# Packed bfloat16 masks, head constants loaded late, and the filter's decay formed on the chip

## The reference, cut to what matters

```python
def _hyena_filter(L, w1, b1, f1, w2, b2, f2, w3, b3, f3, w4):
    t01 = t / max(L - 1, 1)
    z = concatenate([t01[:, None], cos(ang), -sin(ang)], axis=-1)
    h = sin(f1 * (z @ w1 + b1)); h = sin(f2 * (h @ w2 + b2)); h = sin(f3 * (h @ w3 + b3))
    h = h @ w4                                        # (256, 2048)
    deltas = abs(linspace(min_decay, max_decay, HYENA_W))   # (1024,)
    window = exp(-t01[:, None] * deltas[None, :])     # (256, 1024)
    return h * tile(window, (1, 2))

def _block(s, mod, s0_f, s0_b, p):
    sh_a, sc_a, g_a, sh_f, sc_f, g_f = mod            # silu(c) @ w_mod + b_mod
    h = rmsnorm(s, norm_pre_mix) * (1.0 + sc_a) + sh_a
    out, s_f, s_b = mixer(h, s0_f, s0_b, p)           # conv_qkv, a_log, dt_bias, gdn_norm, conv_hy, hyena filter
    s = s + g_a * rmsnorm(out, norm_post_mix)
    h = rmsnorm(s, norm_pre_ffn) * (1.0 + sc_f) + sh_f
    return s + g_f * rmsnorm((silu(h @ w_gate) * (h @ w_up)) @ w_down, norm_post_ffn)
```

## Time and profile before

| | us |
|---|---|
| median of 3 runs | 1673.58 |
| lowest and highest | 1664.75, 1673.95 |
| the profiled execution: its time | 1674.84 |
| its span in the profile | 1673.2 |

### The profile page before, as it was taken

The page is one execution under the profiler, slowest core; times in us unless marked ns, Lnnn a source line. Parts: engine busy times, 40 slices in busy tenths (PEclk is TensorE's granted clock), DMA queues, the critical chain, the costliest instruction groups (busy, mean ns, idle before and its releaser), DMA issues.

```text
span 1673.2 us, 27006 instructions
## 1 busy us (share of the span) xinstructions
PE 1633.6 (98%) x10110; PEld 1410.9 (84%) x10110; DVE 1151.5 (69%) x1701; ACT 769.7 (46%) x1281; POOL 116.6 (7%) x214
## 2 busy tenths in 40 slices
PE   8899999999999999999999999999999999999998
PEld 3257899899998999999998888888888888888886
DVE  4645889899899987776777555555555555665665
ACT  1346564655645556433446444444444444334331
POOL 2000110111101010000110000000000000111110
PEclk9999999999999999999999999999999999999999
DMA  9995353443534445224993344454454456877872
GB/s 360 422 380 211 124 178 132 139 171 127 182 134 138 162 142 183 101 99 156 332 349 123 151 189 167 195 201 166 185 201 178 174 200 224 283 248 248 279 260 94
DMA packets 83305, 334.06 MB, mean 200 GB/s; under 512 B 8120, under 2 KB 24585, under 8 KB 56778
## 3 DMA queue, kind: packets, MB, share of 16 engines
q1 hardware_dynamic: 62592, 258.25, 41.9%
q0 software_dynamic: 19504, 68.20, 12.2%
q10 hardware_dynamic: 1114, 6.34, 1.0%
HBM read 328.56 MB, written 4.19 MB: 199 GB/s over the span
## 4 chain that ended last, share of the span: by engine, by line
PE 84%; DMA 7%; DVE 5%; ACT 2%; issue 1%; DVEq 1%; SPq 0%; ACTq 0%
PE g L485 10%; PE o L485 10%; PE o L478 8%; PE o L479 8%; PE o L480 8%; PE g L486 5%; PE o L486 5%; DMA w_mod_tile_o<-in_w_mod_t 4%; DMA w_mod_raw<-in_w_mod_t 3%; PE g L561 2%; PE o L492 2%; PE g L492 2%; PE o L493 2%; PE g L494 2%; PE o L494 2%; PE g L493 2%
## 5 line engine op out<-in xcount | busy, mean ns | idle before, releaser
L459 DVE TENSOR_TENSOR w_lo<-w_raw,w_hi 128x2048 fp32r<-128x2048 f32 x203 | 464.8, 2290 | 210.7 <-ACT w_hi L454 210.4
L454 ACT CAST w_hi<-w_raw 128x2048 fp32r<-128x2048 f32 x204 | 389.8, 1911 | 222.9 <-PE o L494 73.9
L478 PE MATMUL o<-h_hi,w_hi 128*128 128x256 f32 (+1 forms) x896 | 298.1, 333 | 3.2 <-DVE w_lo L459 1.8
L480 PE MATMUL o<-h_hi,w_lo 128*128 128x256 f32 (+1 forms) x896 | 282.3, 315 | 0.0
L479 PE MATMUL o<-h_lo,w_hi 128*128 128x256 f32 (+1 forms) x896 | 282.1, 315 | 0.0
L485 PE MATMUL g<-h_hi_lo,w_hi 128*128 128x512 f32 x704 | 249.7, 399 | 0.0
L485 PE MATMUL o<-h_hi_lo,w_hi 128*128 128x512 f32 x688 | 245.2, 399 | 0.8 <-DVE h_hi_lo L1973 0.8
L486 PE MATMUL g<-h_hi_lo,w_lo 128*128 128x256 f32 x704 | 198.0, 281 | 0.0
L486 PE MATMUL o<-h_hi_lo,w_lo 128*128 128x256 f32 x688 | 193.5, 281 | 0.0
L478 PEld LDWEIGHTS o<-h_hi,w_hi 128*128 128x128 f32 x896 | 171.5, 191 | 13.8 <-issue 6.4
L480 PEld LDWEIGHTS o<-h_hi,w_lo 128*128 128x128 f32 x896 | 171.0, 191 | 11.0
(11 more groups left out here) (384 smaller groups left out, 2811.7 us busy)
## 6 DMA issues: line engine op xcount, KB each, us to landing
w_raw<-in_w_ff_t SPq DMA_DIRECT2D x88, 1024.0 KB, 6.3
w_raw<-in_w_heads_t SPq DMA_DIRECT2D x56, 1024.0 KB, 4.9
w_mod_raw<-in_w_mod_t SPq DMA_DIRECT2D x32, 1024.0 KB, 12.4
w_raw<-in_w_down_t SPq DMA_DIRECT2D x32, 1024.0 KB, 6.9
w_mod_piece_h<-in_w_mod_t POOLq DMA_DIRECT2D x112, 256.0 KB, 3.6
w_raw<-in_w_out_t SPq DMA_DIRECT2D x16, 1024.0 KB, 8.5
w_mod_tile_o<-in_w_mod_t POOLq DMA_DIRECT2D x16, 1024.0 KB, 9.8
w_mod_piece_d<-in_w_mod_t POOLq DMA_DIRECT2D x64, 256.0 KB, 5.9
```

Of the source, the lines that this page charges most:

```text
L454: e.copy(whi[p.split[j]][:], raw[p.raw[j]][:]).then_inc(hi_ready, 1)
L459: e.tensor_tensor(wlo[p.split[j]][:], raw[p.raw[j]][:], whi[p.split[j]][:].bitcast(F32), ALU.subtract).then_inc(lo_ready, 1)
L478: e.matmul(o, a, xh, start=first, stop=False)
L480: return e.matmul(o, b, xh, start=False, stop=last)
```

## The change

- The 13 masks come as bfloat16 packed two to an fp32 word, half the bytes (416 KB instead of 832), and straight into `lev`. DVE's cast is gone, as are `levf`, `lev_ready` and SP's wait for it. The load moves on POOL's queue behind the four `w_mod_raw_h` tiles, and DVE waits for it (`lev_in`) at the end of `first_dve`.
- The head constants (without the second `gdn_norm`) move on POOL's queue from the start to behind `mod_used` 32, ahead of `w_mod_raw_h`. ACT waits for all six before the gates' tanh, DVE behind the gates tile's `split_lo`; DVE's halving of `gdn_norm` moves there too. `consts_in` counts two loads.
- The window `c_win` (1 MB) is no longer loaded. In its place the 1024 rates (4 KB, one partition) and 256 negated times (8 bytes per partition) come on ACT's queue, ahead of `filt_w4`. TensorE waits for them ahead of its first `spin` and spreads the rates over the partitions with two fp32 matmuls of one row (ones times rates); ACT forms the window with four exponentials whose scale is the time; DVE waits for `win_ready` before the first product with the taps.

```diff
--- before.py
+++ after.py
@@ -128,7 +128,9 @@
     m = levels_mask()
     pairs = m | m.transpose(0, 2, 1)
     blocks = np.stack([np.where((i // s) % 2 == 0, i >= j, i <= j) for s in LEVELS[1:]])
-    c["c_lev"] = np.concatenate([pairs, blocks]).transpose(1, 0, 2).astype(f).copy()
+    masks = np.concatenate([pairs, blocks]).transpose(1, 0, 2).astype(f)
+    halves = (masks.view(np.uint32) >> 16).astype(np.uint16)
+    c["c_lev"] = np.ascontiguousarray(halves).view(np.float32)
     c["c_sq"] = np.stack([i == j, i <= j, i >= j, np.ones((P, P), bool)]).transpose(1, 0, 2).astype(f).copy()
     t = np.arange(SEQ, dtype=np.float64)[:, None]
     w = 2 * np.pi * (np.arange(SEQ, dtype=np.float64)[None, :] + 0.5) / (2 * SEQ)
@@ -144,8 +146,8 @@
     c["c_pos"] = z.T.copy()
     hi, lo = np.log(1e-2) / 0.3, np.log(1e-2) / 1.5
     deltas = np.abs(np.linspace(lo, hi, HY_CH, dtype=f))
-    win = np.exp(-t01[:, None] * deltas[None, :]).astype(f)
-    c["c_win"] = win.reshape(2, P, HY_CH).transpose(1, 0, 2).copy()
+    c["c_times"] = (-t01).reshape(2, P).T.copy()
+    c["c_rates"] = deltas.reshape(1, HY_CH).copy()
     return c
 
 
@@ -170,7 +172,6 @@
         whi.append(at("w_hi_extra", 156, [P, TILE], F32R))
         wlo.append(at("w_lo_extra", 132, [P, TILE], F32R))
         lev = at("lev", 120, [P, 13, P], BF16)
-        levf = at("lev_f32", 140, [P, 13, P])
         sq = at("squares", 124, [P, 4, P])
         tabs = at("tabs", 126, [P, 7, NCHUNK, 2 * HEADS])
         gt = at("g_tok", 123.25, [P, NCHUNK, 2 * HEADS])
@@ -244,6 +245,8 @@
         ab = at("taps_sum_diff", 48, [P, 2, 2, HY_CH])
         kri_f = [at(f"k_re_im_front{part}", kb, [P, 2, 4, SEQ]) for part, kb in enumerate((132, 148))]
         win = at("window", 80, [P, 2, HY_CH])
+        wrates = at("window_rates", 32, [1, HY_CH])
+        wtimes = at("window_times", 0, [P, 2])
         fv = at("filter_v", 207.0625, [FW, 8])
         kri = at("k_re_im", 32, [P, KT_N, TOK])[:, :, SEQ:]
         dft = at("dft", 80, [P, 4, 2, SEQ])
@@ -289,7 +292,7 @@
         DN = Phase("down", 44, 1, split=[1, 0] * 22, loads=[2 if q in (2, 5, 8) else 1 for q in range(DN_TILES)] * 4)
         st = Stream([GA, H0, Hf, H, HT, W0, W, Fa0, Fa, Fb, DN])
         st.plan()
-        N_CONST = 10
+        N_CONST, N_HEAD_CONST = 2, 6
         in_order = lambda a, p, first: (A[a], [first + j for j in range(p.n)], p.n)
         of_heads = lambda h: [7 * (h + 1) + j for j in range(3)] + [7 * h + j for j in range(3, 6)]
         src = {"gates": in_order("w_gates_t", GA, 0), "head0": in_order("w_heads_t", H0, 0),
@@ -302,12 +305,13 @@
         kri_d = nc.dram_tensor("k_re_im_spilled", (P, KT_N, SEQ), F32, kind="Internal").ap()
         landed = [sem(f"raw_landed{s}") for s in range(RAW_SLOTS)]
         hi_ready, lo_ready, w_used = sem("w_hi_ready"), sem("w_lo_ready"), sem("w_tile_used")
+        head_consts_in = sem("head_consts_in")
         c_in, consts_in, res_in, stored = sem("c_in"), sem("consts_in"), sem("res_in"), sem("stored")
         x_in = [sem(f"x_in{j}") for j in range(4)]
         cs_ready, cs_act, xsq_done, xsum_done, xn_done = sem("c_ready"), sem("c_act"), sem("x_squared"), sem("x_summed"), sem("x_normed")
         xsq_used, xsum_rows = sem("x_sq_used"), sem("x_sum_rows")
         mod_landed = [sem(f"mod_landed{s}") for s in range(len(mraw))]
-        lev_ready = sem("lev_ready")
+        lev_in, rates_in, rates_pe, win_ready = sem("lev_in"), sem("window_rates_in"), sem("window_rates_spread"), sem("window_ready")
         mod_used, rows_out, rows_t, mod_cols = sem("mod_tile_used"), sem("mod_rows_out"), sem("mod_rows_t"), sem("mod_cols")
         mpiece_landed, mtile_landed, dpiece_landed = ([sem(f"mod_{n}_landed{s}") for s in range(c)]
                                                       for n, c in (("head", 3), ("out", 2), ("down", 4)))
@@ -647,7 +651,7 @@
             if s == 0:
                 pe.wait_ge(fl_act, 3)
                 pe.wait_ge(filt_pad, 1)
-                pe.wait_ge(filt_in2, 16 * 4)
+                pe.wait_ge(filt_in2, 16 * 3)
             if s >= 3:
                 pe.wait_ge(fl_dve, s + 1)
             pe.matmul(G[3 + s % 3][:, :], fm[:, 0, t * P:(t + 1) * P], fw[:, 3 * FW + n * 512:3 * FW + (n + 1) * 512],
@@ -861,6 +865,11 @@
                                      start=(j == 0), stop=(j == 3))
                 last.then_inc(first_used, 1)
 
+            pe.wait_ge(c_in, 32)
+            pe.wait_ge(rates_in, 32)
+            for n in range(2):
+                last = pe.matmul(G[1 + n][:, :], ONES[0:1, :], wrates[:, n * 512:(n + 1) * 512], start=True, stop=True)
+            last.then_inc(rates_pe, 1)
             def spin(n):
                 for _ in range(n):
                     pe.matmul(G[5][:, :], ONES, sq[:].rearrange("p s n -> p (s n)"), start=True, stop=True)
@@ -1083,14 +1092,20 @@
             act.dma_start(fw[0:EMB, 0:FW], A["filt_w1"]).then_inc(filt_in, 16)
             act.dma_start(fm[0:EMB, 3], A["c_pos"]).then_inc(filt_in, 16)
             act.dma_start(fv[:], A["filt_v"]).then_inc(filt_in, 16)
+            act.dma_start(wrates[:], A["c_rates"]).then_inc(rates_in, 16)
+            act.dma_start(wtimes[:], A["c_times"]).then_inc(rates_in, 16)
             act.dma_start(fw[0:FW, 3 * FW:3 * FW + 2 * HY_CH], A["filt_w4"]).then_inc(filt_in2, 16)
             act.dma_start(hb0[:], A["hyena_bias"]).then_inc(filt_in2, 16)
-            act.dma_start(win[:], A["c_win"]).then_inc(filt_in2, 16)
             act.dma_start(dft_f[:], A["c_dft"][:, 0:2]).then_inc(filt_in2, 16)
             act.wait_ge(c_in, 32)
             act.activation(cvec[:, 1], cvec[:, 0], ACT.Tanh, scale=0.5).then_inc(cs_act, 1)
             for k in range(0, KT_N, 4):
                 act.dma_start(xc[:, k:k + 4], A["xc_t"][:, k:k + 4]).then_inc(x_in[k // 4], 16)
+            act.wait_ge(rates_pe, 1)
+            for t in range(2):
+                for n in range(2):
+                    last = act.activation(win[:, t, n * 512:(n + 1) * 512], G[1 + n][:, :], ACT.Exp, scale=wtimes[:, t:t + 1])
+            last.then_inc(win_ready, 1)
             def rows_evac(m):
 
                 act.wait_ge(mod_used, 4 * m + 4)
@@ -1148,6 +1163,7 @@
 
             refill(act, split_hi, GA, 0, 0)
             act.wait_ge(gates_dve, 1)
+            act.wait_ge(head_consts_in, 16 * N_HEAD_CONST)
             act.activation(gb[0:16, 0], G[2][0:16, :TOK], ACT.Tanh, scale=0.5)
             act.activation(gb[32:48, 0], G[2][32:48, :TOK], ACT.Identity, bias=small[32:48, 1:2])
             act.activation(small[32:48, 4:5], small[32:48, 0:1], ACT.Exp)
@@ -1623,6 +1639,8 @@
 
             t, n = s // 4, s % 4
             v.wait_ge(fl_pe, 4 + s)
+            if s == 0:
+                v.wait_ge(win_ready, 1)
             v.tensor_tensor(filt[:, t, n * 512:(n + 1) * 512], G[3 + s % 3][:, :], win[:, t, (n % 2) * 512:(n % 2 + 1) * 512],
                             mulv).then_inc(fl_dve, 1)
 
@@ -1684,9 +1702,7 @@
             for s in range(8):
                 filter_taps_dve(v, s)
             v.wait_ge(consts_in, 16 * N_CONST)
-            v.tensor_copy(lev[:], levf[:]).then_inc(lev_ready, 1)
             filter_sums_dve(v)
-            v.tensor_scalar(small[:, 3:4], small[:, 2:3], 0.5, None, mulv)
             mod_columns(0)
             v.wait_ge(xsum_done, 1)
             v.tensor_scalar(rr[:, 1], G[2][:, :], 1.0 / D, EPS, mulv, addv)
@@ -1714,6 +1730,8 @@
             v.drain()
             v.memset(gb[0:48], 0.0).then_inc(gates_dve, 1)
             refill(v, split_lo, GA, 0, 0)
+            v.wait_ge(head_consts_in, 16 * N_HEAD_CONST)
+            v.tensor_scalar(small[:, 3:4], small[:, 2:3], 0.5, None, mulv)
             v.wait_ge(gates_act, 1)
             v.tensor_scalar(gb[0:16, 0], gb[0:16, 0], 0.5, 0.5, mulv, addv)
             v.scalar_tensor_tensor(out=gb[32:48, 1], in0=gb[32:48, 0], scalar=0.0, in1=gb[32:48, 1], op0=ALU.max, op1=addv)
@@ -1786,6 +1804,7 @@
                     conv_silu(0, t)
                     if t == 0:
                         gates_dve2(5)
+                v.wait_ge(lev_in, 16)
                 v.wait_ge(rows_t, 9)
                 v.tensor_tensor(modc[:, 0, 48:52], G[4][:, 0:8:2], bmod[:, 48:52], addv)
 
@@ -2061,21 +2080,20 @@
             g.dma_start(fw[0:FW, 2 * FW:3 * FW], A["filt_w3"]).then_inc(filt_in_w, 16)
             g.dma_start(vec[:], A["norms_t"]).then_inc(consts_in, 16)
             g.dma_start(bmod[:], A["b_mod_t"]).then_inc(consts_in, 16)
-            g.dma_start(levf[:], A["c_lev"]).then_inc(consts_in, 16)
-            g.dma_start(taps[:], A["conv_qkv_t"]).then_inc(consts_in, 16)
-            g.dma_start(hytaps[:], A["conv_hy_t"]).then_inc(consts_in, 16)
-            g.dma_start(hybias[:], A["conv_hy_b_t"]).then_inc(consts_in, 16)
-            g.dma_start(small[32:48, 0:1], A["a_log_t"]).then_inc(consts_in, 16)
-            g.dma_start(small[32:48, 1:2], A["dt_bias_t"]).then_inc(consts_in, 16)
```

(13 more changed lines are left out.)

## The result

| | before | after |
|---|---|---|
| median of 22 runs each, us | 1674.14 | 1679.98 |
| lowest and highest | 1663.61, 1677.83 | 1672.96, 1691.06 |
| the profiled execution: its time | 1674.84 | 1691.06 |
| its span | 1673.2 | 1689.4 |

The changed kernel is slower: ratio 1.0046, interval 1.0028 to 1.0065, which is 7.7 us (4.7 to 10.9). Forecast were +4.1 us and 1677.6 us in a range of 1668.5 to 1684.0; the median lies in the range, the direction and the place are as said, and the size is about twice the forecast (7.7 us between the means; the medians differ by 5.8). The profiled execution of the changed kernel happens to be the longest of its 22, so the traces are compared here stage by stage, not by their ends.

What follows compares the result with a forecast made beforehand. The front was held bound by TensorE's list, then DMA landings; the rest by TensorE. Delay 8.1 less capped gain 3.95 gave +4.1 us: 1678.9 for the profiled execution, 1677.6 for the median, range 1668.5 to 1684.

Steps and rivals of the forecast that it cites:

- S: Delay of the start of TensorE's list, from the rates' wait and the spread: 8.1 us, bounds 5.4 and 13.7.
- The hole: Sign in the front: the DMA share falls well under 1 somewhere between 39 and 65 us, where it was full.
- The forecast's own case: Whole front later because TensorE starts late: shift +4.1 us, case counted from +1.4 to +6, chance 0.60.
- the rival of the longer wait: ACT's ring waits for large blocks of SP's ring: rates land at 12.5 to 15 us, shift +6.2 to +8.7, chance 0.15.
- First failed term: TensorE's start: rates land at 10.5 us, eleven packets per engine taking 2.7 to 3.6 us behind `filter_v` on ACT's ring.
- the upper bound of 14.5 us: Latest landing of the rates, if their packets fall into the slow DMA stretch from 8 to 13 us, 0.65 us each.
- The rival of the full saving: Rates land before 6.4 us at the start, so the saved bytes show: shift -1.6 us, 1673.2 us, chance 0.12.
- Second failed term: Spread at TensorE's start: four more passes at the fast pace, 4 x 0.45 = 1.8 us.
- the bound of 3.4 us: Upper price of the spread at TensorE's start: four passes all slow without shortening the slow pace behind them.
- The cap of 3.95 us: Most the second half of the front can gain: tile 16 lands at earliest at 67.2 us, against 71.16.
- The edits at nothing: Exponentials on ACT, dropped mask cast and its wait, later head constants and masks on POOL's queue: all hidden, costing nothing.
- The rival of the late constants: Head constants, wanted by ACT at 128.9 us, land at 133 instead of 125: about 4 us on top, chance 0.05.

Runs made afterwards that it cites:

- e1: The changed kernel with the loads of rates and times first on ACT's queue instead of fourth and fifth; ratio to the kernel before 1.0009.
- e4: The kernel before with only the window formed on the chip as in the changed kernel, masks and head constants loaded early; ratio to the kernel before 1.0047.
- after_again: The changed kernel, unchanged, profiled a second time; 1683.85 us in one execution.
- best: The changed kernel with rates' loads first on ACT's queue, spread behind the first spin, spins cut from 8 to 6 and 6 to 4 matmuls; 1671.38 us.
- e7: The changed kernel with the spread behind the first spin, the second spin cut to 4, the rates' wait still ahead of everything; 1672.24 us in one execution.
- e2: The changed kernel with the rates' wait and the spread behind the first spin, the second spin cut from 6 to 4; ratio to the kernel before 1.0012.
- e6: The kernel before with a first spin of 10 full-row matmuls instead of 8; 1667.54 us in one execution.
- e3: The changed kernel's masks and head constants alone, window loaded whole as before, no rates, spread or start wait; ratio to the kernel before 0.9991.
- e5: The kernel before with two one-row fp32 matmuls of 512 columns ahead of the first spin; 1666.02 us in one execution.

## Why the prediction was right, and where its size was off

**The structure held.** The forecast's formula was: tile 16 lands S - 3.95 us later. Taking S from tile 0's use (32.87 - 20.16 = 12.71 us in the changed kernel), it gives +8.76; the trace has 79.97 - 71.16 = +8.81. It does as well elsewhere: e1 has S 4.48, formula +0.53, trace +0.54; e4 13.55, +9.60, +9.5; after_again 12.11, +8.16, +8.1; best -0.52, -4.47, -4.5. It is off by 1.0 us in e7 (S 7.82, +3.87, trace +4.8) and by 1.7 in e2 (-0.27, -4.22, trace -2.6). The hole, the fast landing of tile 15 after its issue (4.9 us, forecast 4.8) and TensorE as the pace setter are all there. What was mis-sized is S: 12.7 us instead of 8.1.

That the median still lies near the forecast is in part luck. The forecast's own case ended at a shift of +6; the front shifted by 8.8 us at tile 16 and 9.9 at tile 30, which in size is the rival of the longer wait (+6.2 to +8.7, chance 0.15), and a little beyond it. The medians differ by only 5.8 us because of how the runs fell into two groups, told at the end of this section.

**First failed term: the rates land at 12.85 us, not 10.5.** The step was "eleven packets: 2.7 to 3.6 us" behind `filter_v`. The counts were about right. The rings of the changed kernel (packets, MB, share) in the microseconds 6-7, 7-8, 9-10 and 11-12, the last with its line of packet sizes:

```profile
q1 hardware_dynamic: 64, 0.40, 97.6%
q10 hardware_dynamic: 51, 0.00, 2.9%
...
q1 hardware_dynamic: 48, 0.39, 90.8%
...
q10 hardware_dynamic: 49, 0.00, 2.8%
...
q1 hardware_dynamic: 52, 0.30, 78.7%
q0 software_dynamic: 47, 0.06, 16.7%
q10 hardware_dynamic: 49, 0.00, 3.1%
...
DMA packets 32, 0.25 MB, mean 246 GB/s; under 512 B 2, under 2 KB 2, under 8 KB 2
...
q1 hardware_dynamic: 17, 0.14, 57.8%
q10 hardware_dynamic: 15, 0.11, 41.3%
```

ACT's ring moves 49 small packets in a microsecond next to 48 of SP's 8 KB ones: three per engine and microsecond, a pace of 0.33 us, as forecast. A third ring, POOL's (q0), which the forecast left out, moved 34 packets from 7 to 8 us and 47 from 9 to 10, with a share of up to 16.7%. By 11 us nearly all small packets were through. But the landing is marked only at 12.85 us, and packets under 512 B still came, two from 11 to 12 us and one from 12 to 13. I take these three for the load's last ones, on the slowest of the 16 engines; no view names their load. By then `filt_w4`, the next load on the ring, was running beside them, and in that stretch the engines are full at two thirds of the rate before it:

```profile
6.00:11.00 5.00, 0.00 (x0) 0.00 (x0) 1.36 (x9) 0.79 (x2) 0.00 (x0) 1.00 1.04 393
11.00:15.00 4.00, 2.02 (x3) 1.01 (x4) 0.00 (x0) 0.00 (x0) 0.00 (x0) 1.00 0.99 258
```

The forecast saw this slow stretch at 8 to 13 us and used it only for the upper bound of 14.5 us. It had not asked to what it belongs; it starts where `filt_w4`'s 64 rows of 8 KB start, at 8 us before and at 11 in the changed kernel. So my average (packets over rate) gave the time at which most packets were through, and not that of the last. That the landing lies at the rival's edge (12.5 to 15 us) doesn't make its mechanism right. The Trainium skill (DMA: Bandwidth & Descriptors, Queues, rings and completion order) has an engine drain some 9 to 17 descriptors of one ring before it turns to the next. The trace disagrees, if a packet of the profile, here one row of 8 KB, is one descriptor: in the five stretches of 0.2 us from 7 to 8 us SP's ring moved 10, 10, 9, 11 and 8 packets and ACT's 11, 10, 8, 11 and 9, which is turns of about one packet. The rival of the full saving needed a landing before 6.4 us. e1 shows what it takes: 4.94 us when the loads are first on the ring. What set the small load's time was its place in the ring, not a fixed cost.

**Second failed term: the spread, 3.9 us instead of 1.8.** From first matmul to tile 0 the changed kernel needs 19.89 us, before 15.98; e1 needs 19.56, e4 20.22. The step was "if the slow passes are a stretch of time after the idle start, four more passes cost four at the fast pace". That is right for full rows (e6: 1.5 us) and wrong for one row. Even the bound of 3.4 us ("all slow without shortening what follows") was a little too low: the four passes took 3.75 us. TensorE's weight loads in the changed kernel:

```profile
12.95 0.49 PEld L871 LDWEIGHTS g<-window_rates,squares 1*128 1x128 f32 x2 [12.95 <-issue]
13.97 0.33 PEld L871 LDWEIGHTS g<-window_rates,squares 1*128 1x128 f32 x1 [0.52 <-issue]
...
16.66 0.50 PEld L875 LDWEIGHTS g<-squares 128*128 128x128 f32 x2 [1.50 <-issue]
...
21.94 0.24 PEld L875 LDWEIGHTS g<-squares 128*128 128x128 f32 x1 [0.52 <-issue]
22.42 0.19 PEld L875 LDWEIGHTS g<-squares 128*128 128x128 f32 x1 [0.24 <-issue]
```

Rows 0.85 us apart up to 21.94 us, 0.43 apart from 22.42 on: 5.8 us of slow pace behind 16.66, on top of 3.7 before it. The granted clock reads 1.00 all along, so the profile's clock row doesn't show this; the distance between passes does. That 0.85 us is the 1.2 GHz level, as the forecast read it, has support in `best`, where the same distance goes with a granted clock of 0.50 (15 to 17 us).

**The cap of 3.95 us held where the DMA was idle, not always on time.** With TensorE on time, tile 15 landed 6.5 us after its issue in e2 and 6.7 in e3, and 4.9 in best; in e7, with TensorE late, 5.5. So the second half's gain was 2.6 us in e2 (tile 16) and 4.5 in best; what made e2's tile slower was not settled.

**From tile 16 to tile 30 another 1.1 us went.** The forecast had the shift constant; at tile 30 it is +9.9 in the changed kernel, +1.65 in e1 and +10.8 in e4, that is S - 2.8 in all three. The step is between tiles 22 and 23. They land at 94.9 and 98.5 us, 3.6 us apart, against 2.5 before (86.1 and 88.6), and TensorE's weight load waited 0.93 us for the second. An instruction-fetch packet of 1.07 us on one DMA engine falls into 96 to 97 us; the kernel before has one at 60 to 62 us without such a wait. That it is the cause is argued, not shown.

**The edits at nothing were worth nothing.** The exponentials run from 16.77 to 19.19 us while ACT is idle. POOL's queue and ACT's table load in the changed kernel (start, us, engine, line):

```profile
125.43 0.52 POOL L2086 DMA_DIRECT2D small<-in_a_log_t  x1 [120.29 <-PE o L813]
...
128.05 0.61 POOL L2091 DMA_DIRECT2D small<-in_gdn_norm_t  x1
...
134.90 0.54 POOL L2096 DMA_DIRECT2D lev<-in_c_lev  x1
140.18 1.28 ACT L1167 ACT_TABLE_LOAD   x1
```

The last head constant lands 6.9 us after its issue, at 134.9, and ACT is at the gates at 140.2: a margin of 5 us, against 3 to 6 forecast. Both POOL's first issue behind tile 31 and ACT's table load are 11.3 us later than in the earlier trace rows, so the landing answers to 123.6 us on the forecast's scale (123 to 126). The masks land 11.2 us after 134.90, at 146.1, and are wanted at 173. The rival of the late constants falls, by this row and by e3.

**From the front to the end.** The front explains 9.9 us of the difference. In the profiled executions 16.2 us lie between the two kernels, in the two repeats 5.0. The rest is not the change. One piece is TensorE's clock behind the modulation tiles. The changed kernel at tiles 30 and 31 (granted clock 0.94 from 100 to 120 us and 0.89 from 120 to 140):

```profile
118.39 1.93 PE L813 MATMUL o<-w_mod_raw,c_padded 128*32 128x512 f32 x8 [0.26 <-DMA w_mod_raw<-in_w_mod_t]
...
120.84 0.63 PE L483 MATMUL g<-h_lo,w_hi 128*128 128x512 f32 x1
...
125.31 0.39 PE L484 MATMUL g<-h_hi,w_lo 128*128 128x512 f32 x1
```

The matmuls run half as fast for some microseconds after waits on DMA, and how long that lasts differs: from tile 30 to the first head the executions take 52.3 us (six of them), 53.7 to 53.9 (three) or 55.1 to 55.2 (three), the changed kernel 55.1 and 52.3, the kernel before 53.7 and 53.9. Another 5.0 us between the first two profiles lie between the first head and the SwiGLU (773.2 against 768.2 us); the repeats have 769.2 and 772.2, the other way round.

The larger part of the spread is in the SwiGLU. The same group of matmuls on the pages of the changed kernel and of e5 (busy us, mean ns of one):

```profile
L489 PE MATMUL g<-h_hi_lo,w_hi 128*128 128x512 f32 x704 | 249.7, 399 | 0.0
```

```profile
L485 PE MATMUL g<-h_hi_lo,w_hi 128*128 128x512 f32 x704 | 245.0, 391 | 0.0
```

An execution has the one pace or the other over the whole SwiGLU: its 44 products span 486.5 us at 399 ns, 477.2 us in the three executions with 391 to 394 ns (e5, e6, e7), 9.3 us less. That is the size of the gap of 9 us that the three runs of before had shown and the prediction couldn't place. Sorted, the 22 runs of before lie in two groups, 6 from 1663.6 to 1667.8 and 16 from 1673.1 to 1677.8; those of after 11 from 1673.0 to 1678.3 and 11 from 1681.7 to 1691.1. Within either group the changed kernel's mean is 9.4 to 10.0 us higher, close to the trace's 9.9; by that reading the medians differ by 5.8 and the means by 7.7 because the groups were filled unequally. That the groups are the two paces is an inference from their distance, since only profiled executions show the pace; e5 to e7 are low by it, and their ends are therefore not compared with the others'.

## What to carry to other kernels

Taking bytes out of a full DMA pays only as far as the issue of the next tile allows, and a wait put ahead of the first instruction of an engine that paces the slots is paid in full: price the wait first, the bytes after. Put the few bytes that an early instruction needs first on their ring, ahead of any large or many-rowed load. Put matmuls of one row behind the warming matmuls, not ahead of them, and look at the pace of the passes behind them too: two kernels kept it and a third lost it for four passes. When a load has to be timed, ask when its last completion on the slowest engine comes and what runs beside it then, not when the average engine is through.

## What the runs showed of the hardware that was not expected

- A load of 1 KB in, by the counting above, 144 packets took 9.3 to 10.4 us to land as fifth on its ring (changed kernel, its repeat, e4, e7) and 3.5 us as second, with only the rates' 4 KB ahead of it (e1).
- Two fp32 matmuls of one row ahead of the warming matmuls ran at the slow pace, the full ones behind them stayed slow for another 3.4 to 6.1 us, and they cost 2.85 to 4.2 us; two with full rows cost 1.5 us. Two of one row behind the warming took 1.9 us, and in one of three kernels (best) another 1.7 us, in a stretch with a granted clock of 0.57 behind them.
- While a load of 64 rows of 8 KB ran, the 16 engines moved 215 GB/s or 258 GB/s (after) at a full share, against 393 to 422 in the stretches around; the slow stretch moved with that load from 8 to 11 us.
- The 512-column matmuls of the SwiGLU run at 399 or, in other executions, at 391 to 394 ns, worth 9.3 us; what decides it stays open.
